# A two-layer trunk on one core: most products with the weights standing and 256 tokens moving

## What is computed

```python
def pool_layer(x, norm_g, w_in, w_pool, pool_scale, w_out):
    h = rms_norm(x, norm_g)
    u, z = jnp.split(h @ w_in, 2, axis=-1)          # 2048 each
    y = pool_mixer(u, w_pool, pool_scale) * jax.nn.silu(z)
    return x + y @ w_out

# pool_mixer: 4 groups of 512 features, causal windows w = 2, 4, 8, 16
#   pooled = (sum of the last w tokens) / min(pos, w) - u ;  mixed = pooled @ w_pool[group]

def moba_layer(x, norm_g, w_in, q_norm, k_norm, w_out):
    h = rms_norm(x, norm_g)
    q, k, v, z = jnp.split(h @ w_in, 4, axis=-1)    # 2048 each, 16 heads of 128
    q, k = rope(rms_norm(heads(q), q_norm)), rope(rms_norm(heads(k), k_norm))
    o = moba_attention(q, k, v)                     # 256 tokens are one block: plain causal attention
    return x + (o * jax.nn.silu(z)) @ w_out
```

## Time and profile before

| | |
|---|---|
| median of 3 runs | 464.44 us (463.4 to 465.15) |
| span of the profiled execution | 464.1 us |
| time of the profiled execution beside the runs | not given apart from its span; the span lies 0.3 us under the median |
| PE (matmul) busy | 438.2 us, 94% |
| PE weight loads | 366.8 us, overlapping with the matmuls |
| VectorE, ScalarE, GpSimd busy | 257.4, 213.1, 139.7 us |
| weights and inputs moved | 75.6 MB, 163 GB/s over the span |

### The profile page before, as it was taken

The page is one execution under the profiler, slowest core; times in us unless marked ns, Lnnn a source line. Parts: engine busy times, 40 slices in busy tenths (PEclk is TensorE's granted clock), DMA queues, the critical chain, the costliest instruction groups (busy, mean ns, idle before and its releaser), DMA issues.

```text
span 464.1 us, 5733 instructions
## 1 busy us (share of the span) xinstructions
PE 438.2 (94%) x2068; PEld 366.8 (79%) x2068; DVE 257.4 (55%) x335; ACT 213.1 (46%) x273; POOL 139.7 (30%) x125
## 2 busy tenths in 40 slices
PE   6999999999999999999699995999959999599997
PEld 5788888888888888888588884888848888488885
DVE  4967363638774555455356564376634656364542
ACT  4285445453553534455345554356532664444410
POOL 3490000000000001498211884026860268800000
PEclk8999999999999999999799998999979999979999
DMA  7989557464546653567334544435343552522002
GB/s 257 389 282 323 191 167 285 138 224 155 209 153 189 202 178 95 180 187 234 124 92 106 175 133 142 142 119 181 101 170 96 175 173 98 181 92 90 1 0 90
DMA packets 38160, 75.63 MB, mean 163 GB/s; under 512 B 1536, under 2 KB 1664, under 8 KB 38144
## 3 DMA queue, kind: packets, MB, share of 16 engines
q1 hardware_dynamic: 38000, 75.40, 49.5%
q10 hardware_dynamic: 144, 0.02, 0.0%
HBM read 74.37 MB, written 1.05 MB: 163 GB/s over the span
## 4 chain that ended last, share of the span: by engine, by line
PE 57%; POOL 24%; issue 10%; DVE 5%; ACT 1%; DMA 1%; POOLq 1%; SPq 0%; ACTq 0%
PE acc L593 17%; PE acc L595 17%; PE acc L594 17%; POOL wide L344 5%; POOL qk_rstd L326 4%; POOL wide L348 4%; POOL wide L320 3%; PE aux L626 3%; POOL k_s L337 3%; POOL qk_mean L323 3%; DVE w_lo L836 1%; DVE hT_lo L846 1%; DVE k_s L972 1%; POOL qk_rstd L332 1%; DMA raw<-in_w_in_dram 1%
## 5 line engine op out<-in xcount | busy, mean ns | idle before, releaser
L818 DVE TENSOR_TENSOR w_lo<-raw,w_hi 128x2048 fp32r<-128x2048 f32 x65 | 151.7, 2348 | 47.6 <-ACT w_hi L371 43.5
L593 PE MATMUL acc<-w_hi,hT_hi 128*128 128x512 f32 x368 | 148.6, 404 | 0.5 <-DVE w_lo L836 0.5
L595 PE MATMUL acc<-w_hi,hT_lo 128*128 128x512 f32 x368 | 145.0, 394 | 0.0
L594 PE MATMUL acc<-w_lo,hT_hi 128*128 128x512 f32 x368 | 144.8, 394 | 0.0
L371 ACT ACTIVATE w_hi<-raw 128x2048 fp32r<-128x2048 f32 x64 | 122.3, 1915 | 28.5 <-PE acc L595 28.5
L595 PEld LDWEIGHTS acc<-w_hi,hT_lo 128*128 128x128 f32 x368 | 70.0, 190 | 15.2
L593 PEld LDWEIGHTS acc<-w_hi,hT_hi 128*128 128x128 f32 x368 | 70.5, 191 | 14.5 <-DVE w_lo L836 0.6
L594 PEld LDWEIGHTS acc<-w_lo,hT_hi 128*128 128x128 f32 x368 | 70.4, 191 | 13.9
L593 PE MATMUL acc<-w_hi,aT_hi 128*128 128x512 f32 x160 | 64.6, 404 | 0.0
L595 PE MATMUL acc<-w_hi,aT_lo 128*128 128x512 f32 x160 | 63.1, 395 | 0.0
L594 PE MATMUL acc<-w_lo,aT_hi 128*128 128x512 f32 x160 | 63.0, 394 | 0.0
(11 more groups left out here) (107 smaller groups left out, 471.7 us busy)
## 6 DMA issues: line engine op xcount, KB each, us to landing
raw<-in_w_in_dram SPq DMA_DIRECT2D x46, 1024.0 KB, 5.4
raw<-in_w_out_dram SPq DMA_DIRECT2D x16, 1024.0 KB, 5.0
raw<-in_w_pool_dram SPq DMA_DIRECT2D x4, 1024.0 KB, 6.8
raw<-in_w_in_dram SPq DMA_DIRECT2D x8, 256.0 KB, 6.1
wide<-in_xT_dram SPq DMA_DIRECT2D x4, 256.0 KB, 5.9
xs<-in_x_dram SPq DMA_DIRECT2D x1, 1024.0 KB, 8.6
out_dram<-ysb SPq DMA_DIRECT2D x4, 256.0 KB, 2.1
k_s<-in_pool_table_dram SPq DMA_DIRECT2D x1, 288.0 KB, 11.0
```

Source lines behind the costliest of these rows:

```text
L593: pe.matmul(a, shi, whi, start=first and k == 0, stop=False)
L594: pe.matmul(a, shi, wlo, start=False, stop=False)
L595: ins = pe.matmul(a, slo, whi, start=False, stop=last and k == GK - 1)
L818: dve.tensor_tensor(w_lo[:, slot, :], raw[:, slot, :], w_hi[:, slot, :].bitcast(F32), ALU.subtract).then_inc(w_split, 1)
```

## The change

- **Feature-major products.** u, z, the mixing, both output products and the gate of layer 1 now hold a 128 x 128 tile of the weights standing and move 256 tokens (`tile`, L555). A granule is 48 matmuls of 256 columns where it was 24 of 512. 44 of the 68 granules are so: 2112 matmuls. q, k and v keep the old form (`token_major`, L690): 24 granules, 576 matmuls. The results of the 44 are feature-major already, so pooled u, y0, x1 and the attention's output are not turned by TensorE any more; the final output leaves feature-major and is laid out by the host.
- **Pooling** is by shifted sums on GpSimd (`window_sums`, L290): 1 to 4 additions of [128, 4 x 256] for a group. VectorE scales, subtracts u and takes the rest.
- **The token factor** 1/rms lies along the moving side there, so it is spread over the partitions once a layer by a small matmul with a diagonal matrix (`spread_rstd`, L616), and VectorE multiplies u and z with it while evacuating them.
- **q and k** stay in PSUM: ScalarE squares them from there (L479), and VectorE multiplies them from PSUM with both rotation tables (`rope_parts`, L1025). GpSimd adds the two parts, makes the head factors and scales k (`rope_sum`, L322). `turn_qk(g, 1)` stands one granule earlier, behind the first granule of the gate.
- **The probabilities** are normalised by VectorE before TensorE turns them (`probs_norm`).
- **The first two granules** are split by ScalarE and VectorE (GpSimd did the first part before); the weights lie in HBM in granule order, so a partition's 8 KB are in one piece.
- **The loops are unrolled**; waits are on constants.

The core of the diff:

```diff
+            def tile(out_, slot, width, f, count, src, k0, start, stop, ready=None):
+                for k in range(count):
+                    c = k * width + f * P
+                    whi, wlo = w_hi[:, slot, c:c + P], w_lo[:, slot, c:c + P]
+                    if ready:
+                        ready(k0 + k)
+                    pe.matmul(out_, wlo, src[:, k0 + k, 0, :], start=start and k == 0, stop=False,
+                              skip_group_check=True)
+                    pe.matmul(out_, whi, src[:, k0 + k, 0, :], start=False, stop=False, skip_group_check=True)
+                    ins = pe.matmul(out_, whi, src[:, k0 + k, 1, :], start=False, stop=stop and k == count - 1,
+                                    skip_group_check=True)
+                return ins
...
-            def pool_tokens(g, first):
...
-            def turn_y0(g):
...
-            def turn_x1(half):
...
-            def turn_y1(g, after_q):
...
+            def spread_rstd(i):
+                pe.wait_ge(diag_made, i + 1)
+                for t in range(TT):
+                    ins = pe.matmul(banks[6][:, t * P:(t + 1) * P], ones[:, :], diag[:, t, :], start=True, stop=True)
+                ins.then_inc(rstd_spread, 1)
...
+                token_major("v", g, 1, 0)
+                turn_qk(g, 0)
+                pe.wait_ge(parts_made, 4 * g + 4)
+                pair(NUMBER["gate", g, 0], 2)
+                turn_qk(g, 1)
+                pair(NUMBER["gate", g, 1], 3)
+                attend(g, 0)
...
+            def window_sums(g):
...
+                for level in range(g + 1):
+                    shift, dst = 1 << level, sums[level % 2]
+                    chain.done(pool.tensor_tensor(dst[:, :, EDGE:], src[:, :, EDGE:],
+                                                  src[:, :, EDGE - shift:PADDED - shift], ALU.add))
...
+            def rope_sum(g, i):
+                pool.wait_ge(parts_made, 4 * g + 2 * i + 2)
+                ins = pool.tensor_tensor(qk[i], qk[i], turned, ALU.add)
...
+            def rope_parts(g, i, t):
...
+                dve.tensor_tensor(q4, a4, rope_tab[:, 2 * i, t, :].unsqueeze(1).to_broadcast([P, HPG, HEAD_DIM]),
+                                  ALU.mult)
+                for a, b in ((0, half), (half, 0)):
+                    sin = rope_tab[:, 2 * i + 1, t, a:a + half].unsqueeze(1).to_broadcast([P, HPG, half])
+                    ins = dve.tensor_tensor(t4[:, :, a:a + half], a4[:, :, b:b + half], sin, ALU.mult)
```

More of the change, by code:

```diff
@@ L74, with done @@
 class Chain:
     def __init__(self, eng, sem):
[L78 to L80 removed]
+        self.eng, self.sem, self.made = eng, sem, 0
+    def done(self, ins):
         ins.then_inc(self.sem, 1)
         self.made += 1
[L83 to L92, removed]
@@ new lines, in _ @@
+            for n in range(RING, N_END):
+                if n == RING:
+                    sp.wait_ge(piece_split, 4)
+                elif n == RING + 1:
+                    sp.wait_ge(half_split, 2)
+                else:
+                    sp.wait_ge(w_split, splits(n - RING))
+                sp.dma_start(raw[:, n % RING, :], weights[n]).then_inc(raw_landed[n % RING], 16)
+            for f in range(KD):
+                sp.wait_ge(out_made, f // 2 + 1)
+                sp.dma_start(out[f * P:(f + 1) * P, :], xT[:, f, :]).then_inc(out_stored, 16)
@@ L669, in layer0 @@
-            def layer0(g, first):
-                for j in range(2 if first else 0, 4):
-                    granule(4 * g + j, j, j // 2, None, hT_hi, hT_lo, GK * (j % 2), first=j % 2 == 0, last=j % 2 == 1,
-                            halves=first and j == 2)
-                    if j == 2:
-                        pool_tokens(g, first)
-            layer0(0, first=True)
-            with pe.Fori(1, GROUPS) as g:
-                layer0(g, first=False)
-            def turn_y0(g):
-                pe.wait_ge(y0_made, g + 1)
-                if g >= 2:
-                    pe.wait_ge(y_split, 2 * (g - 1))
-                turn((2 * (g % 2), 2 * (g % 2) + 1), ysb[:, g % 2], y_turned)
@@ L687, in _ @@
-            pe.wait_ge(ident_made, 1)
-            pe.wait_ge(pooled_split, 2 * GROUPS)
-            for g in range(GROUPS):
-                free = (y0_made, g - 1) if g >= 2 else ((u_made, gate_made)[g], TT * GROUPS)
-                granule(N_POOL + g, g, g % 2, free, aT_hi, aT_lo, HPG * g, first=True, last=True)
-                if g > 0:
-                    turn_y0(g - 1)
-            def turn_x1(half):
-                pe.wait_ge(x1_made, TT * (half + 1))
-                turn((2 * half, 2 * half + 1), xs[:, :, half * COLS:(half + 1) * COLS], h_turned)
@@ L699, in _ @@
-            for half in range(2):
-                for q in range(4):
-                    pe.wait_ge(y_split, 2 * (q + 1))
-                    granule(N_OUT0 + 4 * half + q, q, half, (y0_made, 3 + half), aT_hi, aT_lo, GK * q,
-                            first=q == 0, last=q == 3)
-                    if (half, q) == (0, 0):
-                        turn_y0(GROUPS - 1)
-                    if (half, q) == (1, 0):
-                        turn_x1(0)
+                pe.matmul(banks[7][:, 0:P], zeros, zeros, start=True, stop=True)
@@ L810, in _ @@
+            for j in range(8):
+                _, h, q = GRANULES[N_OUT1 + j]
+                out1(h, q, j)
         @block.vector
@@ L1056 @@
+            y1_out(last, 1)
+            probs_norm(last, 3)
+            y1_rest(last, 1)
+            weight_lo(N_OUT1 + 7)
+            y1_out(last, 2)
+            y1_rest(last, 2)
+            y1_out(last, 3)
+            y1_rest(last, 3)
+            for i in range(4):
+                dve.wait_ge(out1_ready, i + 1)
+                f = slice(2 * i, 2 * i + 2)
+                dve.tensor_tensor(xT[:, f, :], pair_of(i), xT[:, f, :], ALU.add).then_inc(out_made, 1)
 def kernel(**inputs):
```

1518 lines of the change are left out of this document (800 added, 718 removed), and 3 rows, old and new, of the table GRANULES.

## The result

The changed kernel takes 457.56 us in the median (456.07 to 458.68), against 464.79 for the kernel before. The ratio is 0.984, with a 95% interval of 0.982 to 0.987: 7.2 us faster, where 25 us were forecast. The time lies inside the range of 424 to 462, but the gain is less than a third of the forecast. The profiled execution spans 455.0 us.

The account below looks back on a forecast made before the run. TensorE was taken as the bound, with its waits and clock: 464.1 - 14.9 - 18.2 - 11.9 + 3.2 + 3.2 + 1.6 + 12 = 439 us, 5.4% less. The range was 424 to 462 us.

Parts of the forecast that it names:

- What bounds it: Whole kernel: TensorE, busy 94% of the span, is the bound; its waits and granted clock come next.
- TensorE work that goes: Pooling passes and transposes leave TensorE, less a few new passes: -14.9 us.
- The narrow matmuls: Granules: 2112 matmuls of 256 columns at 0.115 us replace 1056 of 512 at 0.227: +3.2 us.
- fixed price: Rival on narrow matmuls: the 14 ns belong to each standing-tile swap at full clock, giving 450 us; 15%.
- the first rival: The fixed price per matmul, 14 ns at full clock for each swap of the standing tile: 450 us; 15%.
- The wait for k: Turn of q and k: TensorE's wait for rotated k goes, -18.2 us, with a margin of only 2 us.
- The clock: Four half-clock stretches, 23.8 us together, go without gaps of 4 to 5 us: -11.9 us.
- New waits: Layer 1 attention: normalised probabilities come late, 3.4 us a group in three groups and 2 us last: +12 us.
- Head: Kernel start: third granule begins later and spreading the token factor waits 1.3 us: +3.2 us.
- transition: Between mixing and output product: TensorE waits for the last y0's products, copy and rest: +1.6 us.
- Shared reading: Rival on narrow matmuls: weight load and stream draw on one read rate, giving 483 us; 13%.
- Loads that don't hide: Rival on narrow matmuls: each load stands in line with the stream, giving about 662 us; 1%.

Follow-up runs that it names:

- e4: Kernel before without GpSimd's products of k with the two rotation tables, so k stays unrotated; 437.71 us.
- e1: Separate kernel of streams of 48 matmuls of one shape, nothing of the layers computed; 0.120 us per matmul of 256 columns, 0.227 of 512.
- e3: Changed kernel with the four small VectorE operations that negate q's head factors done once a group with head 0; 455.70 us.
- e7: Changed kernel with q's two rotated parts added by VectorE instead of GpSimd; 453.84 us.

## Why the prediction was wrong

- **What bounds it:** right. TensorE bound both kernels, and the waits for k and the clock with them were the loss (e4: the median fell by 27.1 us where the two terms said 30.1).
- **TensorE work that goes, -14.9:** not measured alone; the sum closes to 0.1 us with it.
- **The narrow matmuls, +3.2:** this is the first step that failed, and the largest: 10.5 of the 16 us between the forecast's sum of 439 and the span of 455.0. I took the 14 ns over the stream as a charge per column, since the half clock shows none, and added a little jitter: 0.115 us. It is a fixed price of a matmul at full clock: 0.120 us, +13.7. That was the first rival, at 15%. The half clock excluded a fixed number of engine cycles; it did not exclude a fixed time that shows at the full clock only, and I drew the wrong reading from it. So the two large terms of the change cancel: -14.9 for transposes and pooling, +13.7 for twice the matmuls.
- **The wait for k, -18.2:** right, and L721 shows no wait. The margin was not as counted. In groups 1 to 3 it is 4.3 us and not 2 (k is scaled by 271.82, the turn starts at 276.08), in the first group only 0.2 (218.05 and 218.29). The GpSimd rows that I used, 4.0 us for scaling k and 1.1 for the means, were long for a reason that I did not see: in the changed kernel the scalings take 1.04 us each in seven of eight cases, and the means 0.20 when VectorE does not hold them.
- **The clock, -11.9:** the second step that failed; it came to -5.3. Two errors are in it. I tied the stretches to gaps of 4 to 5 us and forecast gaps of 2 us myself, at a place where I then charged only the gap; gaps of 2.4 us brought 3.4 us of half clock each, and 4.7 us of the loss stayed. And I charged half of 23.8 us although TensorE was busy for 19.9 of them (the earlier trace rows has 6.04 of 6.80 us), which counts 1.9 us twice, here and in the waits for k.
- **New waits, +12:** 11.1 in size and at head 3 in place, but by another cause in part. Of the lateness on VectorE, GpSimd's hold on a small operation made 2.2 us (2.33 instead of 0.17); my row for the row maximum (1.0 us) came from a stretch with GpSimd idle.
- **Head +3.2, transition +1.6:** 2.4 and 2.9.
- **The rivals:** fixed price, with its 450, plus 4.7 of clock comes to 454.7, beside a span of 455.0; the smaller errors cancel. Shared reading is excluded by e1. Loads that don't hide did not come.
- **Luck:** the time lies inside the range of 424 to 462 because the range was wide enough for the rivals. The kernel is faster because of the waits for k that went, not because of its narrow matmuls.

## What to carry to other kernels

A matmul's price has a part that does not shrink with its width. Before a matrix product is turned round to save transposes, multiply the number of matmuls that it adds by that part (here 1056 x 13.5 ns = 14.3 us against 14.9 saved), and measure the part with two widths in one stream.

Where TensorE is the bound, a gap can cost more than its length, since the clock may fall with it. Charge the half clock only for the time in which TensorE works, or the idle part is counted twice. Look first for the operation that ends each gap and ask which work stands ahead of it in its engine's list without being urgent; four such moves were worth 20 us here, the large change 7.

## What the runs showed of the hardware that was not expected

- The fixed part of 13 to 14 ns at full clock for a full standing tile, and 6.7 ns for a standing tile of 64 or 32 columns with 256 moving (e1).
- At the half clock the part is not there: the earlier trace rows have 512 columns at 0.427 us.
- Matmuls of 64 and 192 columns with a full standing tile cost 0.112 us each at the full clock, and those of 128 and 192 cost 0.213 at the half clock (e1).
- The same gaps do not always bring the clock down. With gaps of 1.5 and 0.8 us in each of three groups it fell in two of them in e3, and in one of them in e7. Gaps of 1.3 us between mixing and output product never brought it down. What decides is not shown.
- The clock also fell with no gap in the records. In e1 it went to 0.50 at 24.4 us, at the start of the stream of 128 columns and behind that of 64, and came back at 38.1 us, in the stream of 192: 13.7 us in all, while TensorE was busy without a break:

```profile
24.00:37.60 13.60, 13.60 (x67) 13.60 (x67) 0.00 (x0) 0.00 (x0) 0.52 0.00 0
37.60:60.00 22.40, 22.40 (x164) 22.40 (x163) 0.00 (x0) 0.00 (x0) 0.99 0.01 1
```

- VectorE and GpSimd hold each other up on SBUF. A small VectorE operation waited for the end of a GpSimd addition (2.33 us for two elements), a split of weights did so (3.71 instead of 2.29 us), and GpSimd's operations that began during a split waited in turn (3.82 instead of 1.9 us). VectorE's operations on a bank of PSUM went on beside it (L1018: 0.41 us there, 0.42 elsewhere).
